# Mixer A's cached keys: turned on the host, loaded by pages through SyncE

## The reference, cut to what matters

```python
k_g = jnp.where(is_past, cache_a_k[phys, off], gather_rows(ka, i_new))
v_g = jnp.where(is_past, cache_a_v[phys, off], gather_rows(va, i_new))
out_a = attend_selected(qa, k_g, v_g, idx <= qpos[None, :, None])
# attend_selected: scores q.k * DH**-0.5, softmax over the chosen keys, times v
```

## Time and profile before

| | us |
|---|---|
| median of three runs | 2166.15 (2163.22 to 2167.6) |
| the profiled execution | 2170.43 |
| its span, first to last instruction | 2168.6 |
| granted TensorE clock, mean | 0.835 |

### The profile page before, as it was taken

One profiled execution on the slowest core, in us unless ns is written; L12 is line 12 of the kernel. 1 busy time (PEld: TensorE's weight loads), 2 busy tenths in 40 slices (PEclk: granted clock), 3 DMA queues, 4 the chain that ended last, 5 costly groups with the idle time before them and its releaser, 6 DMA issues.

```text
span 2168.6 us, 27262 instructions
## 1 busy us (share of the span) xinstructions
PE 1698.0 (78%) x8774; PEld 1236.0 (57%) x8774; DVE 1602.5 (74%) x3603; ACT 1257.1 (58%) x2751; POOL 635.5 (29%) x657
## 2 busy tenths in 40 slices
PE   7997699776896985996977987975887796765766
PEld 3554565635664654674655765654655665564554
DVE  2455676486699899869896796886898889768444
ACT  1223434226467654667897697874555465446665
POOL 1000000034334344333333333333333433333431
PEclk9998589886898886997998997987896897876666
DMA  7000300179999999999999999996999999999997
GB/s 277 20 17 13 88 1 30 49 284 420 417 414 390 419 418 390 419 379 384 419 419 374 406 400 371 419 411 248 412 368 362 405 370 385 316 417 358 420 420 302
DMA packets 108351, 695.68 MB, mean 321 GB/s; under 512 B 16688, under 2 KB 19120, under 8 KB 31408
## 3 DMA queue, kind: packets, MB, share of 16 engines
q0 software_dynamic: 95376, 674.29, 77.3%
q1 hardware_dynamic: 12832, 19.65, 3.0%
HBM read 690.14 MB, written 3.76 MB: 320 GB/s over the span
## 4 chain that ended last, share of the span: by engine, by line
PE 33%; DVE 30%; DMA 13%; ACT 10%; DVEq 4%; issue 4%; ACTq 3%; POOL 1%; POOLq 0%
DMA region<-in_peer_rows,region 12%; DVE region L1707 11%; DVE xall L1715 6%; PE ps L2244 5%; PE ps L2049 5%; DVEq L1112 4%; ACTq L1096 3%; ACT region L1100 3%; PE ps L1731 3%; PE ps L1996 2%; PE ps L2066 2%; ACT region L1097 1%; DVE region L1443 1%; PE ps L1899 1%; ACT region L1019 1%
## 5 line engine op out<-in xcount | busy, mean ns | idle before, releaser
L693 POOL DMA_INDIRECT region<-in_peer_rows,region x576 | 569.5, 989 | 1404.1 <-PE ps L2244 712.3
L1707 DVE SCALAR_TENSOR_TENSOR region<-region,h_now 128x1024 f32<-128x1024 f32 x576 | 695.7, 1216 | 208.5 <-DMA region<-in_peer_rows,region 191.8
L2244 PE MATMUL ps<-ident,region 128*128 128x128 f32 x3352 | 567.6, 327 | 253.9 <-ACT region L1100 231.8
L2244 PEld LDWEIGHTS ps<-ident,region 128*128 128x128 f32 x3352 | 472.6, 170 | 358.9 <-ACT region L1100 303.0
L1100 ACT ACTIVATE region<-region 128x1024 f32<-128x1024 f32 x419 | 481.3, 1149 | 35.5 <-issue 1.6
L1095 ACT ACTIVATE region<-region 128x1 f32<-128x1 f32 x576 | 114.5, 199 | 353.1 <-DVE region L1707 348.6
L2049 PE MATMUL ps<-w_uk_s,region 128*128 128x512 f32 x544 | 279.8, 640 | 7.1 <-ACT region L960 6.9
L1715 DVE SCALAR_TENSOR_TENSOR xall<-region,xall 128x1024 f32<-128x1024 f32 x157 | 201.8, 1285 | 68.3 <-ACT region L1097 53.3
L1097 ACT ACTIVATE region<-region 128x1 f32<-128x1 f32 x576 | 169.8, 295 | 40.7 <-issue 1.4
L2049 PEld LDWEIGHTS ps<-w_uk_s,region 128*128 128x128 f32 x544 | 100.2, 205 | 82.6 <-issue 73.9
L960 ACT ACTIVATE region<-ps 128x512 f32<-128x512 f32 x136 | 79.5, 585 | 68.7 <-PE ps L2049 66.0
(11 more groups left out here) (393 smaller groups left out, 2577.3 us busy)
## 6 DMA issues: line engine op xcount, KB each, us to landing
region<-in_w_peer_q POOLq DMA_DIRECT2D x16, 1024.0 KB
region<-in_peer_rows,region POOLq DMA_INDIRECT x576
region<-in_w_in POOLq DMA_DIRECT2D x8, 882.0 KB, 14.1
region<-in_w_peer_q SPq DMA_DIRECT2D x8, 512.0 KB, 4.3
region<-in_x_turned SPq DMA_DIRECT2D x5, 512.0 KB, 3.6
region<-in_w_out SPq DMA_DIRECT2D x2, 1024.0 KB, 12.4
region<-in_w_out SPq DMA_DIRECT2D x1, 2048.0 KB, 18.3
out_p_y<-xall SPq DMA_DIRECT2D x4, 512.0 KB
```

Source lines behind the costliest of these rows:

```text
L693: pool.indirect_dma_start(ring[r][:], None, a["peer_rows"], bass.IndirectOffsetOnAxis(ap=experts[:, t, n:n + 1], axis=0)).then_inc(landed[ ...
L1707: v.scalar_tensor_tensor(ring[r][:, 0:D], ring[r][:, 0:D], 1.0, h_now[:], ALU.mult, ALU.mult, accum_out=acts[:, t % 2, n:n + 1]).then_inc( ...
L2244: last = te.matmul(ps[6 + c // 4][:, (c % 4) * P:(c % 4 + 1) * P], ring[r][:, D + c * P:D + (c + 1) * P], ident[:], is_transpose=True, sta ...
```

## The change

The host now hands the key cache over turned within each page: (page, 128 head dims, 128 keys). SyncE loads it, a page at a time, into `kT_s[:, b % 2, :]`, (128 dims, 2048 keys), with the page's number read from `page_idx` into a register, and the batch's eight new keys into `kT_n`, turned by the access pattern (8 elements in each of 128 partitions). There are two such places, by the batch's parity, with a semaphore for each. TensorE has no transposes and ScalarE no copies of keys; column g of before is now every 16th key from g on. The scores of columns 8 to 15 go to `ps[3]`, the others to `ps[5]`. GpSimd loads values as before, at part 14 of 18. A batch has 18 parts over the same 14 steps. The new key rows no longer share the semaphore `a_new` with the new values.

```diff
-        MA, MI, MR, MC, MX = 24, 8, 19, 34, 10
+        MA, MI, MR, MC, MX = 18, 8, 19, 34, 10
...
-        pages[marks("a_init", 0, 1)[0] + AHEAD].extend((("k", 0), ("v", 0)))
+        pages[marks("a_init", 0, 1)[0] + AHEAD].append(("v", 0))
...
-            pages[marks(f"a{b - 1}", 8, 1)[0] + AHEAD].append(("k", b))
-            pages[marks(f"a{b - 1}", 20, 1)[0] + AHEAD].append(("v", b))
+            pages[marks(f"a{b - 1}", 14, 1)[0] + AHEAD].append(("v", b))
...
+            pages_of_k = a["cache_a_k"].rearrange("a (s d) k -> (a s) d k", s=P // PART)
+
+            def load_k(b, g0, g1):
+                s = S[f"k_in{b % 2}"]
+                for g in range(g0, min(g1, NPG)):
+                    page = sp.value_load(page_idx[P // NPG * g:P // NPG * g + 1, b:b + 1], min_val=0, max_val=(NPHYS - 1) * (P // PART))
+                    sp.dma_start(kT_s[:, b % 2, g * P:(g + 1) * P], pages_of_k[ds(page, P // PART), :, :].rearrange("s d k -> (s d) k")).then_inc(s, 16)
+                if g1 > NPG:
+                    sp.dma_start(kT_n[:, b % 2, 0:NT], o["s_a_k"][b * NT:(b + 1) * NT, :].rearrange("t d -> d t"), allow_slow_non_contiguous=True).then_inc(s, 16)
+
             def a_init():
                 hold(sp, S["made"], 4)
-                load_new(k_s, "s_a_k", 0, S["a_new"])
+                load_k(0, 0, NPG + 1)
                 load_new(v_s, "s_a_v", 0, S["a_new"])
...
-                        if j == 9:
-                            hold(sp, S["k_turned"], 5 * (b + 1))
-                            load_new(k_s, "s_a_k", b + 1, S["a_new"])
-                        if j == 21:
+                        if j < 10 and j % 2 == 0:
+                            hold(sp, S["a_scored"], 3 * b)
+                            load_k(b + 1, 2 * j, 2 * j + 4)
+                        if j == 15:
                             hold(sp, S["a_weighted"], b + 1)
                             load_new(v_s, "s_a_v", b + 1, S["a_new"])
...
             def mixer_a(b):
-                pe.wait_ge(S["k_in"], 16 * (b + 1))
-                pe.wait_ge(S["a_new"], 32 * (b + 1))
...
+                pe.wait_ge(S[f"k_in{b % 2}"], 16 * (NPG + 1) * (b // 2 + 1))
+                pe.wait_ge(S["q_blk"], b + 1)
+                hold(pe, S["ao_kept"], b)
+                hold(pe, S["ao_scaled"], b)
+                if b in (0, NB - 2):
+                    pe.wait_ge(S["y_added"], 3 if b else 2)
+                for q, (g0, n) in enumerate(group_cols(NPG + 1, 4)):
+                    if g0 == NPG:
+                        pe.wait_ge(S["a_evac"], 3 * b + 1)
+                    for g in range(g0, g0 + n):
+                        keys = kT_s[:, b % 2, g::PART] if g < NPG else kT_n[:, b % 2, :]
+                        bank = ps[3] if 8 <= g < NPG else ps[5]
+                        last = te.matmul(bank[:, g % 8 * NTOK:(g % 8 + 1) * NTOK], keys, q_blk[:], start=True, stop=True)
+                    if q in (1, 3, 4):
+                        last.then_inc(S["a_scored"], 1)
+                    yield
+                yield
                 yield
...
+    arrays["cache_a_k"] = _np.ascontiguousarray(arrays["cache_a_k"].reshape(NPHYS, PAGE, KVA * DH).transpose(0, 2, 1))
```

More of the change, by code:

```diff
@@ L255, in program @@
         X = Region(0, X_END)
-        k_s = X.view(NPG + 1, P)
+        kT_s = X.view(2, PAST)
+        kT_n = X.view(2, P)
         v_s = X.view(NPG + 1, P)
-        kT_s = X.view(2, 4, P)
         sa_s = X.view(NPG + 1, NTOK)
@@ L304, in program @@
             "kidx_in0", "kidx_in1", "i_turned", "i_ready", "i_scored", "i_evac", "i_summed", "i_rows", "i_kept", "trial", "counted", "i_chosen", "i_back", "sel_kept",
-            "k_in", "v_in", "q_blk", "k_turned", "k_ready", "a_scored", "a_evac",
+            "k_in0", "k_in1", "v_in", "q_blk", "a_scored", "a_evac",
             "am_part", "am_turned", "am_diag", "am_all", "a_centered", "a_exped", "a_sum", "a_weighted", "ao_scaled", "ao_turned", "ao_kept", "v_lat", "lat_kept")}
@@ L645, in load_batch @@
                     load_pages(kidx[b % 2], a["cache_a_kidx"].rearrange("a (s j) c -> (a s) (j c)", j=PART), b, S[f"kidx_in{b % 2}"])
[L646 to L651, removed]
                 else:
@@ L1043, in mixer_a @@
                 last.then_inc(S["q_blk"], 1)
[L1044 to L1051, removed]
+                for _ in range(11):
                     yield
@@ L1622, in a_init @@
                 dve.wait_ge(S["sel_kept"], 2)
-                v.memset(k_s[:, NPG, :], 0.0)
+                v.memset(kT_n[:], 0.0)
                 v.memset(v_s[:, NPG, :], 0.0)
@@ L1631, in mixer_a @@
             def mixer_a(b):
-                for j in range(12):
+                for j in range(6):
                     for i, (g0, g1) in enumerate(((0, 8), (8, 16), (16, 17))):
-                        if j == (5, 9, 11)[i]:
+                        if j == (2, 4, 5)[i]:
                             n = g1 - g0
@@ L1638, in mixer_a @@
                             v.tensor_tensor(sa_s[:, g0:g1, :].rearrange("p g (h t) -> p g h t", h=HA),
-                                            ps[5][:, 0:n * NTOK].rearrange("p (g h t) -> p g h t", g=n, h=HA), m, ALU.add).then_inc(S["a_evac"], 1)
+                                            ps[(5, 3, 5)[i]][:, 0:n * NTOK].rearrange("p (g h t) -> p g h t", g=n, h=HA), m, ALU.add).then_inc(S["a_evac"], 1)
                     yield
@@ L2129, in mixer_a @@
             def mixer_a(b):
-                pe.wait_ge(S["k_in"], 16 * (b + 1))
-                pe.wait_ge(S["a_new"], 32 * (b + 1))
[L2132 to L2142, removed]
-                            last = te.matmul(ps[5][:, g % 8 * NTOK:(g % 8 + 1) * NTOK], kT_s[:, (q - 1) % 2, g - g0, :], q_blk[:], start=True, stop=True)
-                        if q in (2, 4, 5):
-                            last.then_inc(S["a_scored"], 1)
-                    if q < 5:
-                        g0, n = groups[q]
-                        if q == 0:
-                            hold(pe, S["ao_scaled"], b)
-                            if b in (0, NB - 2):
-                                pe.wait_ge(S["y_added"], 3 if b else 2)
-                        for g in range(n):
-                            last = te.transpose(ps[3][:, g * P:(g + 1) * P], k_s[:, g0 + g, :], ident[:])
-                        last.then_inc(S["k_turned"], 1)
@@ L2155, in mixer_a @@
                     yield
-                    yield
+                yield
                 yield
@@ L2168, in mixer_a @@
                 pe.wait_ge(S["v_in"], 16 * (b + 1))
+                pe.wait_ge(S["a_new"], 16 * (b + 1))
                 for g0, g1 in C_PAGES:
```

## The result

The changed kernel takes 2199.31 us (median of four runs, 2195.67 to 2201.98). Beside it on the same chip the kernel before took 2166.88: **1.0136 times as long, 95% interval 1.0112 to 1.016**, a loss of some 30 us. The forecast was a loss of 8 around 2174, with a range up to 2212. So the sign and the first place of the loss came out as said, and the size was four times too small.

What follows compares the result with a forecast made beforehand. In-order instruction streams bound the stage, DMA close behind. Start +9, strides +9, late keys +5, unhidden DMA +2, gains -17 give +8: 2178.4 us against 2170.43 profiled, 2174 on the runs' median; range 2158 to 2212.

Steps and rivals of the forecast that it cites:

- The turns: DMA engines: each packet of SyncE's queue q1 waits for one big packet of GpSimd's q0, some 0.31 us.
- Start of batch 0, +9: Mixer A's first scores: keys land at 1520 us, TensorE stands 17 us from 1503; costs 9 us, bounds 0 and 17.
- Late keys and rows, +5: Later batches: keys mostly in time, 0 to 13 us late in one batch; 5 us in all with rows landing later.
- Strided weights, +9: TensorE's score weight loads read keys 64 bytes apart: 1.3 us a batch, 9 us for seven.
- The rival "dear": Strided weights on TensorE make each score pair twice as long, 4.8 us a batch: 2198 us; chance 0.1.
- Gains, -17: Dropped TensorE transposes and shorter VectorE waits for ScalarE (L1715) save 2.4 us a batch, 17 us for seven.
- DMA work not hidden, +2: DMA engines: 11 us more work over eight batches against 18.5 us of rest, nearly all hidden; 2 us shows.
- SyncE's issue: SyncE issuing batch 0's key loads with page-number reads, at 1 us each, still ends by 1510 us.
- The rival "SyncE's queue can't keep up": q0's gaps come at wrong times, each of seven batches late, 5 us a batch taken: 2210 us; chance 0.17.

Runs made afterwards that it cites:

- experiments 5: Changed kernel with each batch's 8 new keys loaded as 8 rows of 512 bytes, not element by element: 2186.55 us, 1.007 of the kernel before.
- 3: Changed kernel with a batch's 16 pages loaded by one SyncE DMA from fixed pages, new keys still by elements: 2186.55 us, 1.0072 of the kernel before.
- experiment 1: Changed kernel with scores reading keys side by side in SBUF instead of every 16th key: 2187.82 us, 1.0083 of the kernel before.
- 8: Changed kernel with cached keys by GpSimd in 8 KB rows, new keys as rows, scores reading side by side: 2157.12 us, 0.9921 of the kernel before.
- 2: Changed kernel with cached keys by one GpSimd indirect DMA of 8 KB rows, new keys as rows, stride kept: 2169.69 us, 0.9988 of the kernel before.
- experiment 10: Changed kernel with its 16 page DMAs a batch from fixed pages, no page number read: 2203.05 us, 1.014 of the kernel before.
- experiment 6: Changed kernel with one SyncE DMA for a batch's 16 fixed pages and new keys as 8 rows: 2175.12 us, 1.002 of the kernel before.
- experiment 4: Changed kernel with batch 0's page loads started when the indexer has chosen, new keys' load not moved: 2198.86 us, 1.013 of the kernel before.
- 11: The changed kernel measured again, nothing altered: 2204.24 us, 1.0156 of the kernel before.
- 12: Changed kernel, single run, with score columns in four groups reading keys side by side, 8, 16 and 32 bytes apart: 2201.09 us.
- experiment 7: Changed kernel with one DMA a batch for 16 fixed pages issued by GpSimd, new keys as 8 rows: 2173.69 us, 0.9999 of the kernel before.
- experiment 9: Changed kernel with batch 0's page loads started when keys are chosen and new keys as 8 rows: 2181.29 us, 1.0052 of the kernel before.

## Why the prediction was right or wrong, by its steps

- **The turns** were right and are shown where both queues are full: one packet for one (1919 to 1917), 0.29 us for 0.31, 63.5 us for batch 5's load against 65. The same load took 23 to 38 us in the six batches where q0 had gaps. Keys were expected at 1520 and came at 1523.4, with the whole program 4.3 us late. The rule of the Trainium skill (DMA: Bandwidth & Descriptors, section Queues, rings and completion order) lets an engine drain a packet of some 9 to 17 descriptors from a queue before it turns to the next; the trace here has one 8 KB piece for one 512-byte or 4-byte piece.
- **Start of batch 0, +9**: it cost 15.2 at row 367 and 12 after a few batches. TensorE's idle time was foreseen (17, measured 15.9). The program being 4.3 us late, row 363 (put at 1522.5, came at 1527.83) is only 1.0 us behind the forecast. From the keys to it I had allowed 2.5 us and it took 4.4: the first mask add needs eight columns of scores, 3.7 us on TensorE. Most of what was too kind came after it: the four rows to 367 took 15.1 us, where I had put 3.0 us each, 12.
- **Late keys and rows, +5**: this is the step that failed, by size. 15 instead of 5, and all of it one batch. I had 0 to 13 us of wait for one batch and took 5; it was 14.4, and the whole of it stayed, since VectorE, GpSimd and the ring all stood (VectorE's mask add waits 15.0 us at batch 5). The load took 63.5 us and began 49.2 ahead of its need, at 1701.10 for 1750.28, not 56; the difference is the wait. By experiments 5 and 3 the cause is the number of turns: I had put 70 of the 209 into gaps of q0, and over 1725 to 1760 us (above) there were none.
- **Strided weights, +9**: 11.5 us by experiment 1, 14.5 by 8 against 2. Eight loads take 1.8 us for 0.97, 3.5 us of TensorE for the 34 loads of a batch at the full clock, 28 for eight batches. But 190 of the 272 loads of the changed kernel's scores ran at a granted clock of 0.50, where the stride costs nothing; the other 82 at some 0.12 us make 10 us, near what the experiments show. The rival "dear", 4.8 a batch, is refuted: its price of a load was about right (1.8 times the time), but it holds for the loads at the full clock alone.
- **Gains, -17**: experiment 8 is 17 us faster than before, with the new key rows not turned. That it meets the forecast to the microsecond is partly luck: the shares of it that pay were guesses, and 17 transposes at 0.60 us for four are 2.55 us a batch, not 2.3. The mechanism shows in the changed kernel too. Of its groups of instructions over 1525 to 1875 us this is VectorE's add; it waits 8.6 us for ScalarE, for 25.7 in the earlier trace rows:

```profile
L1711 DVE SCALAR_TENSOR_TENSOR xall<-region,xall 128x1024 f32<-128x1024 f32 x62 | 79.7, 1286 | 14.7 <-ACT region L1093 8.6 <-issue 0.5
```

- **DMA work not hidden, +2**: not tested by itself. The DMA share of the stage went down, 0.94 for 0.95, so it was no bound. (The rest of 18.5 us counted q0 alone; with the other queues the stage stood at 95.4% before, which leaves 16.)
- **SyncE's issue**, said to be done by 1510, took until 1516.4, over 1.2 us a page. By experiment 10 it is not the page number that takes the time; by experiment 6 one DMA with all 2048 pieces is issued in 0.79 us. An earlier start of the 16 DMAs gained nothing (experiment 4). But packets that are handed over in the course of 20 us can't use a gap of 4 us in q0 like those through which the one DMA went in 3 and 6, so the issue is not cleared of a part in batch 0's wait.
- **The rival "SyncE's queue can't keep up"** asked for a wait at each of seven batches and 2210. There was one of 14.4 us, so it is refuted as stated, and my forecast of "one batch" held; yet its mechanism, turns that don't fit into the gaps, is what batch 5 shows, and the time came out between the two.
- The sum as measured in the trace: 4 (not explained) + 12 + 15 and strides against gains, about even: over the five batches between rows 367 and 431 the lag goes from 19.5 to 16.1. That makes 31. By the experiments it is 32 for the transport (2), 14.5 for the stride (8 against 2) and -17 for the gains (8). The transport is the term that I mis-sized: 9, 5 and 2 for it made 16, half of the 32. That the time still lies in the range is owed to the range's width, which was made for the rivals.

**Open**: the 4 us near 740 us, which most of the variants show too; and whether it is mixer B's pages that leave batch 5 no gap. That it is always that batch (experiments 1, 4, 10, 11 and 12 show the same two waits) speaks for the fixed plan and against chance. Open too is how much of 3's and 6's gain is fewer packets and how much the issue at once. Also not run: a version that reads side by side with the values and the mask laid out for it, keys in GpSimd's queue. Experiment 8 has its time but reads the keys in another order than the values have, so the fastest of the complete versions stays the kernel before.

## What to carry to other kernels

Price a load on a second DMA queue in packets, not in bytes: each waits for one packet of the other queue while that queue has work, so beside a full queue of 8 KB rows 209 packets an engine took 63 us while their own work, by the prediction's prices, is 4. Look for where the bulk queue has no gap, since the same load passed in 23 to 38 us where it had some. Count the packets as they come out (a single DMA may join pieces), and hand them over at once, so that a gap can be used. Put no element-wise turned load on such a queue; put the load into the bulk queue, or reduce its count. An earlier start of many small DMAs gained 0 to 3.6 us for 8 here. And a stationary operand may be read up to 8 bytes apart for nothing; from 16 on its load takes 1.6 to 1.7 times as long at the full clock (310 to 335 ns for 192), and nothing more at half of it.

## What the runs showed of the hardware that I had not expected

- Pieces of 512 bytes that one DMA carries for the same partition are moved as 1.8 KB packets in the mean from SyncE's queue (571 for 1.05 MB), and as 4 KB packets from GpSimd's (256 for the same megabyte, experiment 7).
- A small DMA of SyncE behind the 1024 elements can itself be slow to issue: the new values' load after them took 7.76 us in experiment 4 (3.14 in the changed kernel) and 0.30 in experiment 9, where the new keys were rows. (SyncE's timelines; L558.)

```profile
1504.08 7.76 SPq L558 DMA_DIRECT2D region<-out_s_a_v  x1
```
```profile
1503.40 0.30 SPq L558 DMA_DIRECT2D region<-out_s_a_v  x1
```

- The granted clock of the stage fell from 0.84 to 0.79 though TensorE had less to do, 269.7 us for 281.0. In experiments 2 and 8 it was 0.82. Part of the fall lies at the two waits. In each the clock went to 0.50, and it stayed there for 8 to 9 us after the scores had begun (windows as in the earlier trace rows):

```profile
1511.00:1531.00 20.00, 7.55 (x36) 7.55 (x37) 3.68 (x5) 1.65 (x3) 0.94 (x1) 0.50 0.75 272
1753.50:1773.00 19.50, 8.35 (x27) 6.27 (x27) 4.47 (x6) 1.44 (x5) 0.00 (x0) 0.50 0.69 240
```

  I did not test how much of the time the clock made.
